# Attention's divisions by pairs of heads, rotation block by block with the masks loaded earlier, and a reordered finish stage

## The reference, cut to what matters

```python
def _attend(q, k, v, valid, sink):
    s = jnp.einsum('bqgrd,bkgd->bgrqk', q, k).astype(jnp.float32) * (HEAD_DIM ** -0.5)
    s = jnp.where(valid[None, None, None], s, NEG_INF)
    ...
    p = jax.nn.softmax(jnp.concatenate([s, sk], axis=-1), axis=-1)[..., :-1]   # sk: a sink logit per head
    return jnp.einsum('bgrqk,bkgd->bqgrd', p.astype(v.dtype), v)

def _token_mixers(h, p, ck, cv, cstate):
    ...
    attn = _latent_attention(_axial_rope(q), _axial_rope(k), v, ck, cv, sink)   # 8 query heads, 2 kv heads, window +-128
    rw, s_final = _rwkv(rkv, wd, ad, gd, s0, p)    # ends: (layer_norm_by_head(y) * ln_g + ln_b + bonus) * (sigmoid(gd) @ g2)
    out = jnp.concatenate([attn, rw], axis=-1) @ p['w_out']
```

## Time and profile before

| what | us |
|---|---|
| median of 3 runs | 5774.36 (5767.25 to 5780.5) |
| the profiled execution | 5781.65 |
| its span | 5779.5 |
| PE busy | 5403.9 |
| DVE busy | 3242.9 |
| ACT busy | 2192.1 |
| POOL busy | 2129.2 |
| mean granted TensorE clock | 0.968 |

### The profile page before, as it was taken

How to read it: one execution, slowest core, us unless ns; L and a number is a source line. 1 busy time by engine, 2 the same in 40 slices (tenths; PEclk the granted TensorE clock), 3 DMA queues, 4 the chain that set the end, 5 groups by cost and what they waited for, 6 DMA issues and landing times. The chain is left out here.

```text
span 5779.5 us, 117866 instructions
## 1 busy us (share of the span) xinstructions
PE 5403.9 (94%) x47764; PEld 5201.7 (90%) x47764; DVE 3242.9 (56%) x6038; ACT 2192.1 (38%) x2761; POOL 2129.2 (37%) x968
## 2 busy tenths in 40 slices
PE   7977888999999999999988788989999999999999
PEld 4857788999999999999987577889999999999998
DVE  6545558655553156666645564775656622666665
ACT  5433322555556422222242432235555563222221
POOL 0001222656655434343300012236556554333332
PEclk9989999999999999999998899999999999999999
DMA  6100112455555654444421001224555546544443
GB/s 257 61 16 12 62 56 86 140 179 176 180 177 168 219 181 165 169 163 167 138 85 45 18 5 61 88 93 164 178 177 179 178 161 233 172 168 163 167 167 109
DMA packets 303870, 777.73 MB, mean 135 GB/s; under 512 B 23596, under 2 KB 109100, under 8 KB 299368
## 3 DMA queue, kind: packets, MB, share of 16 engines
q1 hardware_dynamic: 303464, 771.94, 39.3%
HBM read 586.52 MB, written 185.34 MB: 134 GB/s over the span
## 5 line engine op out<-in xcount | busy, mean ns | idle before, releaser
L2245 POOL TENSOR_TENSOR ex_v_lo<-ex_v_raw,ex_v_hi 128x1024 fp32r<-128x1024 f32 x256 | 692.7, 2727 | 1070.6 <-ACT ex_v_hi L2151 1070.6
L344 PE MATMUL ex_ps<-tk_h_hi,tk_u_hi 128*128 128x320 f32 x4096 | 964.7, 317 | 43.3 <-POOL tk_u_lo L2233 35.0
L2233 POOL TENSOR_TENSOR tk_u_lo<-tk_u_raw,tk_u_hi 128x1024 fp32r<-128x1024 f32 x256 | 638.0, 2493 | 880.7 <-ACT tk_u_hi L2121 872.2
L344 PE MATMUL ex_ps<-ex_wa_hi,ex_v_hi 128*128 128x320 f32 x4096 | 935.0, 310 | 18.8 <-issue 18.8
L344 PE MATMUL ex_ps<-tk_h_hi,tk_u_lo 128*128 128x320 f32 x4096 | 936.9, 310 | 0.0
L344 PE MATMUL ex_ps<-tk_h_lo,tk_u_hi 128*128 128x320 f32 x4096 | 935.9, 310 | 0.0
L344 PE MATMUL ex_ps<-ex_wa_lo,ex_v_hi 128*128 128x320 f32 x4096 | 934.9, 309 | 0.0
L344 PE MATMUL ex_ps<-ex_wa_hi,ex_v_lo 128*128 128x320 f32 x4096 | 934.6, 309 | 0.0
L2405 DVE TENSOR_TENSOR ex_y<-ex_y,ex_ps 128x640 f32<-128x640 f32 x496 | 406.3, 819 | 670.1 <-PE ex_ps L344 665.9
L344 PEld LDWEIGHTS ex_ps<-tk_h_hi,tk_u_hi 128*128 128x128 f32 x4096 | 678.9, 189 | 45.3 <-POOL tk_u_lo L2233 35.9
L344 PEld LDWEIGHTS ex_ps<-ex_wa_hi,ex_v_hi 128*128 128x128 f32 x4096 | 686.3, 188 | 19.3 <-issue 19.3
(11 more groups left out here) (335 smaller groups left out, 7757.7 us busy)
## 6 DMA issues: line engine op xcount, KB each, us to landing
tk_u_raw<-in_expert_u SPq DMA_DIRECT2D x256, 512.0 KB, 4.3
ex_v_raw<-in_expert_v SPq DMA_DIRECT2D x256, 512.0 KB, 3.5
act_spill<-tk_act_e SPq DMA_DIRECT2D x256, 320.0 KB, 2.3
grid_scratch<-tk_grid SPq DMA_DIRECT2D x160, 512.0 KB, 5.8
ex_g<-grid_scratch SPq DMA_DIRECT2D x64, 1280.0 KB, 10.5
x<-in_w_mod_rows SPq DMA_DIRECT2D x192, 256.0 KB, 4.5
ex_a<-act_spill SPq DMA_DIRECT2D x32, 1280.0 KB, 6.5
x<-act_spill SPq DMA_DIRECT2D x32, 1280.0 KB, 6.4
```

Source lines behind the costliest of these rows:

```text
L344: ins = nc.tensor.matmul(out[:, q, 0:HALF], a, b[:, q * HALF:(q + 1) * HALF], start=(first and n == 0), stop=(last and n == 2))
L2233: nc.gpsimd.tensor_tensor(u_lo[:, at % 2], u_raw[:, at % 3], u_hi[:, at % 2].bitcast(F32), ALU.subtract).then_inc(e["u_split"], 1)
L2245: nc.gpsimd.tensor_tensor(v_lo[h][:, k], v_raw[:, k], v_hi[h][:, k].bitcast(F32), ALU.subtract).then_inc(e["v_split"], 1)
```

## The change

In the rotation stage PE raises `rotated` after each block, in the order k, q0, q1, q2, q3; DVE, POOL (blocks k, q1, q3 for the cosines) and the additions follow block by block. DVE no longer waits for `kv_out`; SP does. The mask table gets memory of its own, and its DMA is issued in the rotation stage, ahead of `kv_out`'s. In the attention stage PE's and ACT's orders stay. DVE's becomes: first pair of masked scores of `part + 2`, divisions of the first pair of `part + 1`, second pair of masked scores and the maxima of `part + 2`, divisions of the second pair of `part + 1`, so that the two small instructions ahead of the divisions are issued for each pair. In the finish stage gates 0 and 2 go to `ps[:, 1]`, the sums to `ps[:, 0]`; the sums follow gate 0; all four widenings follow one another between the attention halves of output blocks 0 and 1; ACT and DVE are ordered to match, and ACT's `weight_high(1)` moves from behind gate 1 to behind gate 3.

```diff
+        mask = sb("mask", [P, TILES, 4 * P])
+        turns, by_pool = (Z_K, 0, 1, 2, 3), (Z_K, 1, 3)
...
+                    sp.dma_start(mask[:], s.d["masks"].rearrange("m p n -> p m n")).then_inc(mask_in, 16)
                     sp.dma_start(s.d["kv_out"][bass.ds(layer, 1)].rearrange("a p b n -> p (a b) n"),
                                  s.z[:, Z_K:Z_V + 1, 0:CTX]).then_inc(kv_out, 16)
+                    sp.wait_ge(mask_in, 16)
                     sp.wait_ge(kv_out, 16)
...
-                    for b in range(5):
-                        last = nc.tensor.matmul(ps[:, b, :], swap[:], s.z[:, b, CTX:T], start=True, stop=True)
-                    last.then_inc(rotated, 1)
+                    for b in turns:
+                        nc.tensor.matmul(ps[:, b, :], swap[:], s.z[:, b, CTX:T], start=True, stop=True).then_inc(rotated, 1)
...
-                    pool.wait_ge(rotated, 1)
-                    nc.gpsimd.tensor_tensor(s.z[:, 3:5, CTX:T], s.z[:, 3:5, CTX:T], bcast(rope[:, 0], 1, 2),
-                                            ALU.mult).then_inc(cos_done, 1)
+                    for n, b in enumerate(turns):
+                        if b in by_pool:
+                            pool.wait_ge(rotated, n + 1)
+                            nc.gpsimd.tensor_tensor(s.z[:, b, CTX:T], s.z[:, b, CTX:T], rope[:, 0], ALU.mult).then_inc(cos_done, 1)
...
-                    link = Chain(dve, chain)
+                    v = nc.vector
+
+                    def sine(n):
+                        dve.wait_ge(rotated, n + 1)
+                        v.tensor_tensor(rot[:, turns[n]], ps[:, turns[n]], rope[:, 1], ALU.mult).then_inc(sin_done, 1)
+
+                    def add(n):
+                        b = turns[n]
+                        dve.wait_ge(sin_done, n + 1)
+                        if b in by_pool:
+                            dve.wait_ge(cos_done, by_pool.index(b) + 1)
+                        else:
+                            dve.wait_ge(cos_own, (n - 1) // 2 + 1)
+                        v.tensor_tensor(s.z[:, b, CTX:T], s.z[:, b, CTX:T], rot[:, b], ALU.add).then_inc(whole, 1)
+
                     for m in (1, 6):
-                        dve_m = nc.vector.memset(k_tiles[:, m, :], 0.0)
-                        link(dve_m)
-                        link(nc.vector.memset(v_tiles[:, m, :], 0.0))
-                    dve.wait_ge(kv_out, 16)
-                    dve.wait_ge(rotated, 1)
-                    link(nc.vector.tensor_tensor(rot[:], ps[:], bcast(rope[:, 1], 1, 5), ALU.mult))
-                    link(nc.vector.tensor_tensor(s.z[:, 0:3, CTX:T], s.z[:, 0:3, CTX:T], bcast(rope[:, 0], 1, 3),
-                                                 ALU.mult))
-                    dve.wait_ge(cos_done, 1)
-                    link(nc.vector.tensor_tensor(s.z[:, 0:5, CTX:T], s.z[:, 0:5, CTX:T], rot[:], ALU.add))
-                    link(nc.vector.tensor_copy(k_tiles[:, 0, :], s.z[:, Z_K, 0:CTX]))
-                    link(nc.vector.tensor_copy(k_tiles[:, 2:6, :].rearrange("p a n -> p (a n)"), s.z[:, Z_K, CTX:T]))
-
+                        v.memset(k_tiles[:, m, :], 0.0).then_inc(keys, 1)
+                        v.memset(v_tiles[:, m, :], 0.0).then_inc(keys, 1)
+                    v.tensor_copy(k_tiles[:, 0, :], s.z[:, Z_K, 0:CTX]).then_inc(keys, 1)
+                    dve.wait_ge(loaded, 64)
+                    sine(0)
+                    for n in (1, 3):
+                        sine(n)
+                        b = turns[n]
+                        v.tensor_tensor(s.z[:, b, CTX:T], s.z[:, b, CTX:T], rope[:, 0], ALU.mult).then_inc(cos_own, 1)
+                        add(n - 1)
+                        if n == 1:
+                            dve.wait_ge(whole, 1)
+                            v.tensor_copy(k_tiles[:, 2:6, :].rearrange("p a n -> p (a n)"), s.z[:, Z_K, CTX:T]).then_inc(keys, 1)
+                        add(n)
+                        sine(n + 1)
+                    add(4)
 
...
-        mask = rot[:].rearrange("p a n -> p (a n)").rearrange("p (m n) -> p m n", m=TILES)
...
-        with stage(nc, "at_mask", "at_scores", "at_masked", "at_negated", "at_top", "at_exp", "at_den", "at_inverse",
+        with stage(nc, "at_scores", "at_masked", "at_negated", "at_top", "at_exp", "at_den", "at_inverse",
                    "at_probs", "at_pt_ready", "at_pt_taken", "at_out", "at_out_taken") as \
-                (block, mask_in, scores, masked, negated, top_ready, exped, den_ready, inverse, probs, pt_ready, pt_taken,
+                (block, scores, masked, negated, top_ready, exped, den_ready, inverse, probs, pt_ready, pt_taken,
                  out_ready, out_taken):
-            @block.sync
-            def _(sp):
-                sp.dma_start(mask, s.d["masks"].rearrange("m p n -> p m n")).then_inc(mask_in, 16)
-
...
-                def front(part):
+                def masked_pair(part, q):
                     sink = s.pvs("sink")[:, PART * (part % 2):PART * (part % 2) + PART]
-                    if part >= SLOTS:
-                        dve.wait_ge(pt_ready, 4 * (part - SLOTS) + 4)
-                    for h in range(PART):
+                    for h in (2 * q, 2 * q + 1):
+                        if part >= SLOTS:
+                            dve.wait_ge(pt_ready, 4 * (part - SLOTS) + h + 1)
                         dve.wait_ge(scores, 4 * part + h + 1)
                         v.tensor_tensor_reduce(sm[:, part % SLOTS, h, :], ps_s[:, h, :], mask[:, part // 2, :], 1.0,
                                                sink[:, h:h + 1], ALU.add, ALU.max, top[:, part, h:h + 1]).then_inc(masked, 1)
+
+                def tops(part):
+                    sink = s.pvs("sink")[:, PART * (part % 2):PART * (part % 2) + PART]
                     dve.wait_ge(masked, 4 * part + 4)
                     v.tensor_scalar(top[:, part], top[:, part], -1.0, None, ALU.mult).then_inc(negated, 1)
                     dve.wait_ge(negated, part + 1)
                     v.tensor_tensor(sink_e[:, part], sink, top[:, part], ALU.add).then_inc(top_ready, 1)
 
-                def back(part):
-                    dve.wait_ge(exped, 5 * part + 5)
-                    v.tensor_tensor(den[:, part], den[:, part], sink_e[:, part], ALU.add).then_inc(den_ready, 1)
-                    dve.wait_ge(den_ready, part + 1)
-                    v.reciprocal(den[:, part], den[:, part]).then_inc(inverse, 1)
-                    dve.wait_ge(inverse, part + 1)
-                    for h in range(PART):
+                def divide(part, q):
+                    pair = slice(2 * q, 2 * q + 2)
+                    dve.wait_ge(exped, 5 * part + 2 * q + 3)
+                    v.tensor_tensor(den[:, part, pair], den[:, part, pair], sink_e[:, part, pair], ALU.add).then_inc(den_ready, 1)
+                    dve.wait_ge(den_ready, 2 * part + q + 1)
+                    v.reciprocal(den[:, part, pair], den[:, part, pair]).then_inc(inverse, 1)
+                    dve.wait_ge(inverse, 2 * part + q + 1)
+                    for h in (2 * q, 2 * q + 1):
                         v.tensor_scalar(sm[:, part % SLOTS, h, :], sm[:, part % SLOTS, h, :], den[:, part, h:h + 1], None,
                                         ALU.mult).then_inc(probs, 1)
...
-                dve.wait_ge(mask_in, 16)
-                front(0)
-                front(1)
+                for part in range(2):
+                    for q in range(2):
+                        masked_pair(part, q)
+                    tops(part)
+                for q in range(2):
+                    divide(0, q)
                 for part in range(N):
-                    back(part)
-                    if part + 2 < N:
-                        front(part + 2)
-                    if part >= 3 and part % 2:
-                        take((part - 3) // 2)
+                    for q in range(2):
+                        if part + 2 < N:
+                            masked_pair(part + 2, q)
+                            if q:
+                                tops(part + 2)
+                        if part + 1 < N:
+                            divide(part + 1, q)
+                    if part >= 2 and part % 2 == 0:
+                        take(part // 2 - 1)
                 take(TILES - 1)
...
+        gate_ps = (ps[:, 1], side[:, 1])
...
-                    if b < 2:
-                        pe.wait_ge(e["centred"], b + 3)
-                    else:
-                        pe.wait_ge(e["gate_g"], b - 1)
+                    if b == 1:
+                        pe.wait_ge(e["centred"], RB)
+                    if b >= 2:
                         pe.wait_ge(e["gated_bonus"], b - 1)
                     for q in range(2):
-                        last = mm(side[:, b % 2, q, 0:HALF], g2[:, b * P:(b + 1) * P], half(gd, q), start=True, stop=True)
+                        last = mm(gate_ps[b % 2][:, q, 0:HALF], g2[:, b * P:(b + 1) * P], half(gd, q), start=True, stop=True)
```

(33 more changed lines are left out.)

4 lines of the change are left out of this document (2 added, 2 removed).

## The result

| kernel | median us (runs) | ratio to the kernel before, 95% interval |
|---|---|---|
| before, same chip | 5773.14 (5767.25 to 5780.5; 4) | |
| changed | 5710.74 (5708.42 to 5713.27; 4) | 0.9893 [0.9881, 0.9906] |
| changed, a second set (before on its chip: 5771.81; 7) | 5717.96 (5712.47 to 5719.66; 4) | 0.9903 [0.9886, 0.9920] |

The forecast was 5713, range 5698 to 5737, "faster". Both sets lie in the range, on either side of 5713. The profiled execution of the changed kernel took 5712.25, with a span of 5710.2 and a mean granted clock of 0.973 (0.968 before).

A forecast was written before the change was run, and what follows sets the result against it. PE, busy 94% of the span, was taken as the bound, so only its waits could shrink. Terms 1.5 + 3.7 + 23.0 + 2.5 = 30.7 per layer, 61.4 for two, from the median 5774.36 gave 5713 us, range 5698 to 5737.

The forecast's parts named there:

- The circle in attention: Attention: PE and DVE take turns, divisions queue behind all four masked scores of a later part; period 8.0 us.
- C: Attention: with divisions by pairs PE sets 6.24 us per part; 23.0 us less per layer, bounds 18 and 24.
- B: Attention's start: masks loaded early, so masked scores follow PE's first scores; 3.7 us less per layer, bounds 3.3 and 4.5.
- A: Rotation stage: DVE starts after the first block; 1.5 us less per layer, bounds 0 and 3.5.
- D: Finish stage: earlier sums and reciprocals under the new order; 2.5 us less per layer, bounds 0 and 5.
- up to 5.0: Finish stage: PE reaches the mixed blocks at about 712 instead of 716.78, a gain of up to 5.0 us.
- DVE as bound: Rival, attention: DVE's 5.85 us of work per 6.24 us part becomes the bound; parts of 7.2, 5728 us; chance 0.15.
- No collisions on POOL: Rival, rotation and finish stages: POOL does not hold up DVE, A 3.5 and D 5; 5704 us; chance 0.12.
- Divisions change nothing: Rival, attention: PE waits on something else in the circle, such as ACT's copies; 5759 us, or 5774; chance 0.03.
- The lower clock holds through attention: Rival, attention: parts take 11.2 us in place of 8.9 at the lower clock; 5805 us; chance 0.02.

The follow-up runs named there:

- 512 columns more: The changed kernel with one more unused DVE addition of 512 columns per attention part, behind the second divisions; 5719.44 us in one run.
- 1024: The changed kernel with one more unused DVE addition of 1024 columns per attention part; median 5721.71 us, ratio 0.9912 to the kernel before.
- the divisions alone: The kernel before with only DVE's new order in the attention stage, masks still loaded at its start; median 5738.15 us, ratio 0.9927.

## Why the prediction was right

**The circle in attention, and C.** Right in mechanism and size. The forecast of 6.24 per part measured 6.22 to 6.23, the waits on divisions fell from 19.9 to 3.1 us, and C came to 23.2 / 22.3 for 23.0. DVE's work was forecast at 5.85 a part and measured 5.77, so the margin of 0.39 was 0.46: as thin as the rival said, but enough. That three tenths of the stage's gain come as a higher clock (8.50 of 27.77), and not as idle time that is gone, is in the sum, since it went by the full clock for every part behind part 0; the prediction does not say how much it is.

**B.** Right in mechanism (first masked score 2.08 behind PE, 2.11 forecast), 0.8 too small. It assumed the lower clock through all of the first scores; PE's denser start had it at full clock by 339.76 (0.92 where the earlier trace rows have 1.65), the case in which I had named 4.5 as the bound.

**A.** Mis-sized, 0.9 and 1.3 for 1.5. That is the one pair of profiles in the table; over all of them it is 1.5, by errors on both sides. What I named as a lower bound and then left out of the value, the mask transfer that delays the cached values' landing, cost 0.8 a layer on the mean. The chain behind PE's first product, forecast at about 13, came out at 13.1 in these profiles but at 12.6 on the mean. Its sum has a slip too: eleven instructions of 0.6 and the copy from 327.35 on end at 334.3, not at 334.65. And the key copy beside POOL took 1.38, where I had 0.35. The Trainium skill ("SBUF — State Buffer", section "Who interferes with whom") says that copies can enter a mode of two ports, in which they and GpSimd block each other as well; the traces agree (1.38 beside POOL in the changed kernel, 0.43 in the run with all products on DVE).

**D.** 2.9 / 1.7 for 2.5, 2.8 over all profiles. The path was right: reciprocals 3.1 earlier, low parts ready at 25.6, 31.5, 33.8 and 36.2 us into the stage where 26.1, 32.3, 34.6 and 37.0 were forecast. The additions took 1.09 and 2.98 and the low parts 1.28 and 2.14, so the collisions were named rightly. One thing doesn't hold: I named them as all that stands in the way of "up to 5.0". With most of them gone PE set the end, at its lower clock behind the widenings, and the first update of x came no earlier.

**The rivals.** DVE as bound: refuted, but only by 0.46 us a part. With 512 columns more DVE is already the slower engine, at 6.36, and with 1024 it sets the parts, at 6.93 (8.5 us more in the two stages). No collisions on POOL: refuted by the rows of 1.76, 2.98 and 2.14. Divisions change nothing: refuted by the divisions alone (0.9927). The lower clock holds through attention: refuted, 1.00 from 349.40 on. With the waits for DVE gone PE has no pauses in parts 1 to 7, and the lower stretches of before's attention, at 0.90 on the mean of the earlier trace rows, are gone too.

**The sum.** Four terms off by up to 0.85 each, on both sides, made 61.4 for 61.4; that it is exact is luck. Over all profiles the same sum is 62.6. 5713 rests as well on subtracting from the median and not from the profiled execution, which lay 7.3 higher.

## What to carry to other kernels

Where two engines take turns, look for the instruction that is queued behind work it doesn't need: to divide a pair of heads as soon as its own exponentials are done moved no work away, added two small instructions to each part, and took 22 us a layer out of the stage: some 16 of them PE's waiting, the rest the higher clock that came with it. Before you trust the new bound, list the other engine's work in a period, and then test the list with a dummy instruction of known length. Read the answer from that engine's own pace: a lead can hide for many parts that it has become the slower one. Work given to GpSimd to relieve VectorE is worth a check of what it does to VectorE's own two-input instructions beside it.

## What the runs showed of the hardware

- The granted TensorE clock fell to 0.74 over 10 us in which PE was busy for 9.92, behind 5.3 us of products with 8 rows; with these in two groups it fell behind the second. A busy PE in the profile was no sign of the full clock there.
- Beside a POOL product of two SBUF tensors single DVE instructions grew by up to most of its length: an addition from 0.82 to 2.98 beside products that take 2.4 alone, another from 0.68 to 1.76 and a copy from 0.43 to 1.38 beside products of 1.27.
- A 1280 KB load issued directly behind four small ones, on the same queue, delayed the first use of the small ones by 0.8 us on the mean, between 0.1 and 1.6.
